# Two block boundaries of a fused two-layer kernel, worked through by token tile

## The reference, cut to what matters

```python
h = x
u = rms_norm(h, norm_mix_pre)
...
h = h + rms_norm(y @ w_out, norm_mix_post)
u = rms_norm(h, norm_mlp_pre)
f = jnp.square(jax.nn.relu(u @ w_mlp_in)) @ w_mlp_out
h = h + rms_norm(f, norm_mlp_post)
...
xn = rmsnorm(h, mix_norm_w)
proj = xn @ w_in
```

## Time and profile before

| | |
|---|---|
| median of 3 runs | 1466.92 us (1465.39 to 1467.94) |
| the profiled execution | 1466.52 us, span 1464.7 us |
| TensorE matmul busy | 1312.1 us (90%), mean granted clock 0.96 |
| TensorE weight load busy | 951.8 us (65%) |
| VectorE, ScalarE, GpSimd busy | 865.5, 477.0, 665.0 us |
| first boundary, 235 to 248 us | TensorE busy 6.97 of 13 us, granted clock 0.74 |
| second boundary, 427 to 445 us | TensorE busy 11.65 of 18 us, granted clock 0.72 |
| 445 to 762 us (mixer, peer query) | TensorE busy 315.71 of 317 us |
| 762 us to the end (experts) | DMA queues busy 0.95, 393 GB/s |

### The profile page before, as it was taken

One profiled execution on the slowest core, in us unless ns is written; L12 is line 12 of the kernel. 1 busy time (PEld: TensorE's weight loads), 2 busy tenths in 40 slices (PEclk: granted clock), 3 DMA queues, 4 the chain that ended last, 5 costly groups with the idle time before them and its releaser, 6 DMA issues.

```text
span 1464.7 us, 17724 instructions
## 1 busy us (share of the span) xinstructions
PE 1312.1 (90%) x6502; PEld 951.8 (65%) x6502; DVE 865.5 (59%) x1712; ACT 477.0 (33%) x817; POOL 665.0 (45%) x392
## 2 busy tenths in 40 slices
PE   5999998999989999999999897887878888777786
PEld 5997987998879999999876563443324443333232
DVE  3234343799325965533627776776777777677654
ACT  3664524443343524122201332222322222222211
POOL 5453236888865623221203444443444445445430
PEclk9999999999989999999999999999899998999989
DMA  7724243445542443132316999999999999999993
GB/s 267 282 83 172 110 172 116 173 173 202 200 172 105 158 170 115 59 115 87 125 49 249 422 422 421 421 421 422 422 421 421 422 421 422 421 422 421 422 421 130
DMA packets 53918, 389.92 MB, mean 266 GB/s; under 512 B 5177, under 2 KB 13513, under 8 KB 14153
## 3 DMA queue, kind: packets, MB, share of 16 engines
q0 software_dynamic: 36864, 268.45, 44.1%
q1 hardware_dynamic: 14432, 116.40, 21.3%
q10 hardware_dynamic: 2536, 3.95, 0.8%
HBM read 387.70 MB, written 1.07 MB: 265 GB/s over the span
## 4 chain that ended last, share of the span: by engine, by line
PE 56%; DMA 28%; DVE 7%; issue 3%; POOL 3%; ACT 1%; ACTq 0%; DVEq 0%; POOLq 0%
PE psum L503 55%; DMA work<-experts_dram,work 18%; DMA weight_ring<-experts_dram,work 8%; DVE work L1685 3%; DMA constants<-experts_dram,work 2%; POOL weight_lo L2160 1%; POOL work L2244 1%; PE psum L633 1%; ACT work L2087 0%; DMA bias_rows_dram<-work 0%; DVE residual L1168 0%; DVE work L1482 0%; POOL norm_stats L2150 0%; POOL weight_ring L2244 0%; PE psum L856 0%
## 5 line engine op out<-in xcount | busy, mean ns | idle before, releaser
L503 PE MATMUL psum<-work 128*128 128x128 f32 (+6 forms) x1880 | 451.3, 396 | 71.7 <-ACT work L2087 71.6
L503 PEld LDWEIGHTS psum<-work 128*128 128x128 f32 (+2 forms) x1880 | 266.0, 193 | 246.2 <-issue 148.3
L2160 POOL TENSOR_TENSOR weight_lo<-weight_ring,weight_hi 128x2048 fp32r<-128x2048 f32 x64 | 299.6, 4680 | 184.1 <-ACT weight_hi L1757 160.4
L2244 POOL DMA_INDIRECT work<-experts_dram,work x153 | 176.9, 1156 | 221.8 <-PE psum L503 183.4
L1685 DVE CUSTOM_DVE_ANT_0 work<-work 128x1024 f32<-128x1024 f32 x153 | 187.5, 1225 | 107.7 <-DMA work<-experts_dram,work 95.3
L503 PE MATMUL psum<-weight_ring,work 128*128 128x512 f32 (+1 forms) x448 | 199.8, 591 | 33.1 <-ACT work L2087 33.1
L503 PEld LDWEIGHTS psum<-weight_ring,work 128*128 128x128 f32 (+1 forms) x448 | 81.5, 186 | 138.3 <-issue 82.8
L503 PE MATMUL psum<-normed_T,weight_ring 128*128 128x256 f32 (+1 forms) x768 | 158.1, 365 | 3.0 <-ACT normed_T L1757 3.0
L1757 ACT ACTIVATE weight_hi<-weight_ring 128x2048 fp32r<-128x2048 f32 x66 | 125.9, 1915 | 88.5 <-PE psum L503 48.0
L503 PEld LDWEIGHTS psum<-normed_T,weight_ring 128*128 128x128 f32 x768 | 137.2, 193 | 24.1 <-issue 5.3
L2087 ACT ACTIVATE work<-constants,work 128x128 f32<-128x128 f32 x256 | 103.2, 403 | 148.6 <-DVE work L1699 142.3
(11 more groups left out here) (261 smaller groups left out, 1717.5 us busy)
## 6 DMA issues: line engine op xcount, KB each, us to landing
weight_ring<-weights_dram SPq DMA_DIRECT2D x50, 2048.0 KB, 7.9
work<-weights_dram SPq DMA_DIRECT2D x3, 1024.0 KB, 6.5
work<-experts_dram,work POOLq DMA_INDIRECT x153, 20.9
weight_ring<-weights_dram SPq DMA_DIRECT2D x2, 1024.0 KB, 13.3
gain_rows<-gains_dram SPq DMA_DIRECT2D x2, 1024.0 KB, 10.2
work<-bias_rows_dram ACTq DMA_DIRECT2D x2, 1024.0 KB, 10.6
weight_ring<-experts_dram,work POOLq DMA_INDIRECT x80, 19.6
constants<-constants_dram ACTq DMA_DIRECT2D x1, 1094.0 KB, 9.5
```

The lines of the kernel that those rows point to most:

```text
L503: return nc.tensor.matmul(o, l, r, start=start, stop=stop)
L2160: G_.tensor_tensor(low, loaded, high.bitcast(F32), ALU.subtract).then_inc(S("weight_lo_ready"), 1)
L2244: G_.indirect_dma_start(out=slots[s], out_offset=None, in_=experts, in_offset=bass.IndirectOffsetOnAxis(ap=expert[:, n % UNIT_BUFS, i:i + ...
```

## The change

It takes both boundaries apart by token tile.

- The last slab before a boundary (the second half of `w_out`; the last two halves, 14 and 15, of the MLP's second product) is multiplied for tile 0 first, with both of its weight halves, then for tile 1.
- `tile_boundary` replaces `transposes` and the first `split_features` after it. TensorE transposes tile 0, multiplies the first bank (256 features) of the next projection for tile 0, transposes tile 1, multiplies the second bank for tile 0, then both banks for tile 1. These matmuls have 128 moving columns in place of 256, so the slab has 192 in place of 96.
- In each of these groups all products with u's high part come before those with its low part, so the former wait for ScalarE alone (`u_hi_ready`) and the latter for VectorE (`drained`).
- The banks of the transposes hold four chunks of one tile each, so ScalarE's copies and VectorE's `scalar_tensor_tensor`s have 128 columns, twice as many as before; the mixer's drains keep their size of 512.
- The `rstd`s, squares and drains of each engine are ordered by tile. Half 23's low part (`MLP_HALF + 1`) moves from GpSimd to VectorE, between tile 0's `add_branch` and its diagonal. Half 55's (`QKV_HALF + 1`) moves ahead of the second boundary on VectorE, its high part likewise on ScalarE, and `mixer_scale` gets memory of its own for it. Half 24's high part comes after the drains.

The diff, cut to its core:

```diff
-DVE_HALVES = (5, QKV_HALF + 1)
+DVE_HALVES = (5, MLP_HALF + 1, QKV_HALF + 1)
...
-    mixer_scale = view(work, 12384, TT, P)
+    mixer_scale = view(work, 29712, TT, P)
...
+            def tile_transposes(name, src, norm, scale, t):
+                pe.wait_ge(S("normed_ready"), TT * norm + t + 1)
+                for j in range(2):
+                    ps = open_bank(name, 2 * t + j)
+                    for a in range(4):
+                        c = 4 * j + a
+                        ins = mm(ps[:, a * P:(a + 1) * P], src[:, t, c * P:(c + 1) * P], scale[:, t, :])
+                    close_bank(ins, name, 2 * t + j)
...
+            def tile_features(name, halves, src, after, highs, t, banks=range(2)):
+                for i in banks:
+                    hi, lo = halves[i]
+                    ps = psum[:, filled[name, i][0], :] if t else open_bank(name, i)
+                    for a in range(2):
+                        f, o = slice(a * P, (a + 1) * P), ps[:, a * SEQ + t * P:a * SEQ + (t + 1) * P]
+                        for k in range(KC):
+                            if i == a == 0 and k % 4 == 0:
+                                pe.wait_ge(S("u_hi_ready"), highs + 2 * t + k // 4 + 1)
+                            mm(o, hi[:, k, f], src[0][:, k, t * P:(t + 1) * P], k == 0, False)
+                            mm(o, lo[:, k, f], src[0][:, k, t * P:(t + 1) * P], False, False)
+                        for k in range(KC):
+                            if i == a == 0 and k % 4 == 0:
+                                drained(pe, after, 2 * t + k // 4)
+                            ins = mm(o, hi[:, k, f], src[1][:, k, t * P:(t + 1) * P], False, k == KC - 1)
+                    if t:
+                        close_bank(ins, name, i)
+            def tile_boundary(branch, norm, scale, name, highs, src=(u_hi, u_lo)):
+                tile_transposes(branch, h_tok, norm, scale, 0)
+                halves = [take_half(), take_half()]
+                tile_features(name, halves, src, branch, highs, 0, (0, ))
+                tile_transposes(branch, h_tok, norm, scale, 1)
+                tile_features(name, halves, src, branch, highs, 0, (1, ))
+                tile_features(name, halves, src, branch, highs, 1)
+                slab_read(name, 1)
...
+                for tiles, part in (((0, ), 0), ((0, ), 1), ((1, ), 0), ((1, ), 1)) if by_tile else ((range(TT), 0), (range(TT), 1)):
+                    if 0 in tiles:
+                        parts.append(take_half())
+                    hi, lo = parts[part]
...
-                split_rows("w_out", mixed_hi, mixed_lo, 512, half * TT, mixed=True)
-            transposes("mlp_T", h_tok, norm=1, scale=mlp_scale)
-            for s in range(8):
-                split_features(f"mlp_in{s}", after=None if s else "mlp_T")
+                split_rows("w_out", mixed_hi, mixed_lo, 512, half * TT, mixed=True, by_tile=half == 1)
+            tile_boundary("mlp_T", 1, mlp_scale, "mlp_in0", 0)
+            for s in range(1, 8):
+                split_features(f"mlp_in{s}")
...
+            for j in range(14):
+                hi, lo = take_half()
+                mlp_half(j, hi, lo, range(TT)).then_inc(S("mlp_out_half_read"), 1)
+                if j % 2:
+                    slab_last.append(("mlp", j + 1))
+            last_halves = [take_half(), take_half()]
+            for t in range(TT):
+                for j in (14, 15):
+                    mlp_half(j, *last_halves[j - 14], (t, ))
+            slab_read("mlp_out", 3)
+            tile_boundary("mix2_T", 2, mixer_scale, "qkv0", 4, (u2_hi, u2_lo))
...
+            branch_gain("w_out", 2, 0, 1, gain_bc[:, 0, :])
+            add_branch(1, "w_out", (0, 2), 0)
+            vector_weight_low(DVE_HALVES[1])
+            scale_diagonal(2, 0, mlp_scale)
+            branch_gain("w_out", 3, 1, 1, gain_bc[:, 0, :])
+            add_branch(1, "w_out", (1, 3), 1)
+            drain_T_low(0)
+            scale_diagonal(2, 1, mlp_scale)
+            drain_T_low(1)
...
+            vector_weight_low(DVE_HALVES[2])
             for half in range(2):
                 branch_gain("mlp_out", half, 0, half, gain_bc[:, 1, :])
             add_branch(3, "mlp_out", (0, 1), 0)
+            scale_diagonal(4, 0, mixer_scale)
             for half in range(2):
                 branch_gain("mlp_out", 2 + half, 1, half, gain_bc[:, 1, :])
-            scale_diagonal(4, 0, mixer_scale)
             add_branch(3, "mlp_out", (2, 3), 1)
-            vector_weight_low(DVE_HALVES[1])
+            drain_mixer_in(0)
             scale_diagonal(4, 1, mixer_scale)
+            drain_mixer_in(1)
...
+            squares(1, 0, full(act, "w_out", 0))
+            squares(1, 2, full(act, "w_out", 1))
+            squares(1, 1, full(act, "w_out", 2))
+            residual_squares(2, "w_out", (0, 2), 0)
+            squares(1, 3, full(act, "w_out", 3))
+            drain_T_high("mlp_T", "g_mlp", 0)
+            residual_squares(2, "w_out", (1, 3), 1)
+            drain_T_high("mlp_T", "g_mlp", 1)
...
-            for h in range(OUT_HALF + 2, MLP_HALF + 2):
+            for h in range(OUT_HALF + 2, MLP_HALF + 1):
                 weight_low(h)
-            for n in (1, 2):
-                for t in range(TT):
+            for t in range(TT):
+                for n in (1, 2):
                     rstd(n, t)
```

More of the change, by code:

```diff
@@ L2174, in _ @@
                 weight_low(h)
-            for n, t in ((3, 0), (3, 1), (4, 0), (4, 1)):
-                rstd(n, t)
+            for t in range(TT):
+                for n in (3, 4):
+                    rstd(n, t)
             drained(pool, "mix2_T", 3)
-            for h in range(DVE_HALVES[1] + 1, SPLIT_HALVES):
+            for h in range(DVE_HALVES[2] + 1, SPLIT_HALVES):
                 weight_low(h)
```

114 lines of the change are left out of this document (49 added, 65 removed).

## The result

| | before | after |
|---|---|---|
| runs | 1466.62 us median of 4 (1465.39 to 1467.94) | 1479.09 us median of 4 (1475.97 to 1480.17) |
| ratio | | 1.0082, 95% interval 1.0067 to 1.0097 |
| profiled execution | 1466.52 us, span 1464.7 | 1479.84 us, span 1478.0 |

A forecast was written before the change was run, and what follows sets the result against it. TensorE was taken to bound the kernel up to the expert stage. First boundary +4.2, second +4.5, clock +3 made +11.7 us on 1466.5, so 1478 us; range 1463 to 1500, own case 1470 to 1482, slower 0.78.

The forecast's parts named there:

- the weight load paces 128-column products: First slab behind each boundary: halving a 256-column product saves nothing, so the split slab costs +11.5 us before any gain.
- A narrow product at 0.120 us: First slabs: a 128-column product takes 0.120 us start to start, as one of 256 columns; 192 take 23.0 us against 11.5.
- First boundary +4.2 us: From `w_out` to the MLP's first slab: transposes start at 236.5, slab ends at 263.8 against 259.65, +4.2 us.
- Stall of 1.4 us in the MLP: Before the second boundary TensorE waits 1.4 us for GpSimd's split of the last weight half, wanted before tile 0 begins.
- VectorE's weight split of 2.29 us now lies in idle time ahead of this boundary and costs nothing.: Second boundary: the weight split moved to VectorE takes 2.29 us, in idle time, and adds 0 us.
- Clock +3 us, falling at 436 and won back behind tile 1's transposes: Second boundary: thin narrow products let the clock fall around 436; tile 1's 16 transpose records win it back; +3 us.
- The rival that the clock stays low to the slab's end: Slab runs slowly after the fall: +20 us instead of +3 at the second boundary, 1495 us; both, about 1515; chance 0.28.
- Cheap narrow products: Rival: first slabs' 128-column products take 0.067 us, the load hidden behind the product before; 1457 to 1460 us; chance 0.18.

The follow-up runs named there:

- widths: Kernel before, four first-projection MLP slabs in products of 128, of 64, of 192 and 64 columns, and of 128 with each weight block used twice; 1641 us.
- late_half: Changed kernel, waiting for the MLP's last weight half only before its own first product, not two groups earlier; 1479.9 us.
- keep_busy: Changed kernel plus 20 thrown-away products of 256 columns in front of three waits of the second boundary; 1477.0 us.
- narrow_alone: Kernel before with only the first slab of both projections in 192 products of 128 columns, still after both tiles' transposes; 1509.2 us.
- narrow_kept: Kernel before with both first slabs in 128-column products, plus thrown-away products in front of the waits of both boundaries; 1527.4 us.

## Why the prediction was right, and where it was not

Sign and size are right (1478.0 for 1479.1 us), and so is the reason: the weight load paces 128-column products. That the size fits so well is in part luck. At the end of the second slab the trace is 9.0 us behind the kernel before (462.63 for 453.61) and the forecast was 11.7; the rest came from places that it did not name. By its steps:

- *A narrow product at 0.120 us.* 0.1115 us (widths, and every full-clock stretch after). 172 of them make 1.5 us a boundary too much. The forecast leaned on how long loads last, too (133 ns for 64 columns, 194 for 128); the same rows have 141 ns for 128 columns, so not those durations but the distance from start to start gives the price. The Trainium skill (TensorE: Matmul & The Clock Gate, LDWEIGHTS) gives 107 ns for such a load by the load's columns alone; the trace has 4% more, and agrees in that 64 and 128 moving columns cost the same. The same page's 81 ns for a stream of 128-column products (Back-to-back issue gap) is not what runs here show.
- *First boundary +4.2 us.* +2.7, the difference being that 1.5 us. Transposes were forecast at 236.5 (235.66), with 1.7 us idle (1.65), at full clock.
- *Stall of 1.4 us in the MLP.* 1.5 us, where it was said to be. late_half shows that removing it alone does not pay.
- *"VectorE's weight split of 2.29 us now lies in idle time ahead of this boundary and costs nothing."* This step failed. The duration came from a row beside which GpSimd splits nothing; beside GpSimd's splits it was 6.04 us and lay on the chain, for 0.5 us here and for all that late_half had gained. The Trainium skill has the rule (GPSIMD Engine Reference, Specifications): GpSimd's way into SBUF is shared with VectorE where that reads two operands from SBUF. The rows agree: the split reads both its operands from SBUF and ended 2.15 us after GpSimd's.
- *Clock +3 us, falling at 436 and won back behind tile 1's transposes.* It fell at 440.0 and came back behind them. keep_busy puts its price at 3.3 us.
- *Not forecast:* the 16-column products (16 of them, in the 32 records that the prediction calls products), +3.2 us at the low clock. The prediction had their fall in its rows and took it as fixed. Whether it is the change that makes it longer is open: late_half, with the same products from there on, reads 68.30 us in C, as before. And +1.1 us behind `xa`, within the scatter there.

So 11.7 forecast, 13.3 in the trace: -1.5 and -0.7 in the two boundaries, +0.3 for the clock, +3.2 for the 16-column products, +0.3 for the two ends.

The rival that the clock stays low to the slab's end, 20 us a boundary, did not happen in the change but did in narrow_alone (second slab, 17.9 us beyond the width's 9.9) and narrow_kept. In the change the slab's own transposes of tile 1 stand between narrow products; whether they brought the clock back was not tried by itself. Cheap narrow products are refuted.

## What to carry to other kernels

Before a product is split so that work can start earlier, compare the piece's time with its weight load: below that, columns are free, and the split doubles the price. Take the duration of an operation from a row in which its neighbours are as busy as they will be, and after removing a wait look who is late next. A stream of narrow products is a risk by itself: in three of these kernels the clock fell in one and came back only when it was over, while the profile shows TensorE fully busy. In others it kept the full clock for a whole slab, so measure more than one execution.

## What the runs showed of the hardware

- Products of this type on 128 stationary columns lie 0.1115 us apart at full clock for 64 and 128 moving columns, 0.213 us at the low one for 64 to 256. A block used twice was loaded twice and saved nothing.
- With TensorE 100% busy by its row the clock fell under 64-column products and stayed at 0.50 for 198 us, and it read 0.50 for 40 us under 128-column ones; other slabs of 128-column ones kept 1.00 for 21 us.
- 16 products of 16 columns in a row cost 0, about 2 or about 5 us of lowered clock besides their own 3.6 us; spread over a slab of wide ones, none.
- A VectorE subtraction of 128 x 2048 elements with both operands in SBUF took 2.29 us alone and 6.04 us beside the same on GpSimd, ending 2.15 us after it; GpSimd's stayed at 4.6. The other way round, a GpSimd step of 0.19 us took 1.80 us beside VectorE's.
